# A mixer, a mixture of experts and two attention layers on one core: the experts' weights used unsplit, in two halves of TensorE's columns

## The reference, cut to what matters

```python
x = x + gt1 * y_x                                   # token mixer
tokens = rms_norm(x, g_norm2) * (1.0 + sc2) + sh2
y = moe_ffn(tokens, ...)                            # 16 experts, 2 for a token
x = rms_norm(x + gt2 * y, g_final)
for l in range(2):                                  # second_block
    x = x + merged(delta, sparse, memory) @ w_out[l]
    x = x + (silu(gt) * up) @ w_ffn_out[l]
return rmsnorm(x, norm_final)
```

## Time and profile before

| | |
|---|---|
| three runs | 2695.44, 2700.69, 2703.59 us, median 2700.69 |
| the profiled execution's own time | 2700.96 us |
| its span in the profile | 2699.1 us |
| busy: PE, DVE, ACT, POOL | 2580.8, 1887.9, 1511.8, 181.7 us |
| moved by DMA | 610.09 MB |
| mixer and routing | to about 448 us |
| experts | about 448 to 1190 us |
| two layers | about 1193 to 2682 us |
| end | to 2699.1 us |

### The profile page before, as it was taken

How to read it: one execution, slowest core, us unless ns; L and a number is a source line. 1 busy time by engine, 2 the same in 40 slices (tenths; PEclk the granted TensorE clock), 3 DMA queues, 4 the chain that set the end, 5 groups by cost and what they waited for, 6 DMA issues and landing times.

```text
span 2699.1 us, 44061 instructions
## 1 busy us (share of the span) xinstructions
PE 2580.8 (96%) x16251; PEld 2173.3 (81%) x16251; DVE 1887.9 (70%) x2149; ACT 1511.8 (56%) x1543; POOL 181.7 (7%) x211
## 2 busy tenths in 40 slices
PE   5999998999999999999999999999999999999997
PEld 3756887878787878879897787899898977878995
DVE  3444767999999999975677575555456785756553
ACT  4433555888888888863556453443345564533432
POOL 0000010000000000000074000000000740000000
PEclk9999998999999999999999999999999999999999
DMA  7434636999999999964433025454544340254545
GB/s 284 161 151 157 225 141 256 400 413 407 408 411 405 411 403 413 403 275 169 156 144 138 34 102 203 172 188 160 193 171 146 140 152 34 102 203 172 188 156 195
DMA packets 79658, 610.09 MB, mean 226 GB/s; under 512 B 16004, under 2 KB 21700, under 8 KB 24968
## 3 DMA queue, kind: packets, MB, share of 16 engines
q1 hardware_dynamic: 79496, 607.87, 58.3%
HBM read 606.79 MB, written 1.05 MB: 225 GB/s over the span
## 4 chain that ended last, share of the span: by engine, by line
issue 48%; PE 33%; DVE 8%; POOL 6%; DMA 2%; ACT 2%; SPq 1%; DVEq 0%; POOLq 0%; ACTq 0%
PE psum_scalar L1801 4%; PE psum_scalar L1802 4%; DVE weight_slabs_rounded L1759 3%; PE psum_vector L550 3%; PE psum_vector L552 3%; PE psum_vector L551 3%; POOL arena L3543 3%; PE psum_scalar L550 2%; PE psum_scalar L551 2%; PE psum_scalar L552 2%; POOL arena L3546 2%; DVE arena_rounded L1759 2%; PE psum_vector L1773 2%; DMA weight_slabs<-in_mixer_slabs 1%; PE psum_scalar L1841 1%
## 5 line engine op out<-in xcount | busy, mean ns | idle before, releaser
L2202 DVE TENSOR_TENSOR weight_slabs_rounded<-weight_slabs,arena_rounded 128x2048 fp32r<-128x2048 f32 x208 | 477.9, 2307 | 342.5 <-ACT arena_rounded L2199 293.2
L2199 ACT ACTIVATE arena_rounded<-weight_slabs 128x2048 fp32r<-128x2048 f32 x208 | 396.4, 1913 | 361.6 <-PE psum_vector L552 223.5
L550 PE MATMUL psum_scalar<-arena_rounded,arena_rounded 128*128 128x256 f32 (+1 forms) x1456 | 472.6, 325 | 20.1 <-DVEq L1294 7.5
L550 PE MATMUL psum_vector<-arena_rounded,arena_rounded 128*128 128x512 f32 (+3 forms) x1264 | 456.2, 361 | 15.0 <-DVE weight_slabs_rounded L2202 14.9
L1759 DVE TENSOR_TENSOR weight_slabs_rounded<-weight_slabs,arena_rounded 128x2048 fp32r<-128x2048 f32 x192 | 430.9, 2285 | 9.0 <-DVE arena L1978 3.9
L1747 ACT ACTIVATE arena_rounded<-weight_slabs 128x2048 fp32r<-128x2048 f32 x192 | 362.2, 1910 | 38.5 <-PE psum_scalar L1802 19.8
L552 PE MATMUL psum_vector<-arena_rounded,arena_rounded 128*128 128x512 f32 (+1 forms) x896 | 348.0, 388 | 0.0
L551 PE MATMUL psum_vector<-weight_slabs_rounded,arena_rounded 128*128 128x512 f32 x880 | 343.8, 391 | 0.0
L550 PEld LDWEIGHTS psum_scalar<-arena_rounded,arena_rounded 128*128 128x128 f32 x1456 | 278.7, 191 | 52.4 <-issue 22.3
L1801 PE MATMUL psum_scalar<-arena_rounded,arena_rounded 128*128 128x512 f32 x768 | 307.9, 401 | 2.7
L550 PEld LDWEIGHTS psum_vector<-arena_rounded,arena_rounded 128*128 128x128 f32 (+2 forms) x1264 | 237.9, 188 | 54.6 <-DVE weight_slabs_rounded L2202 11.5
(11 more groups left out here) (497 smaller groups left out, 4138.8 us busy)
## 6 DMA issues: line engine op xcount, KB each, us to landing
weight_slabs<-in_layer_slabs SPq DMA_DIRECT2D x103, 2048.0 KB, 7.7
weight_slabs<-in_expert_slabs SPq DMA_DIRECT2D x192, 1024.0 KB, 8.2
arena<-in_expert_slabs SPq DMA_DIRECT2D x96, 1024.0 KB, 8.5
weight_slabs<-in_mixer_slabs SPq DMA_DIRECT2D x32, 2048.0 KB, 8.3
weight_slabs<-in_layer_slabs SPq DMA_DIRECT2D x6, 1024.0 KB, 5.5
arena<-in_mem SPq DMA_DIRECT2D x3, 1024.0 KB, 11.9
arena<-in_b_gate SPq DMA_DIRECT2D x6, 512.0 KB, 8.3
arena<-in_x SPq DMA_DIRECT2D x1, 1024.0 KB, 5.2
```

Of the source, the lines that this page charges most:

```text
L550: pe.matmul(out, left[0], right[0], start=start, stop=False)
L2199: e.activation(fr(high), low, ACT.Copy).then_inc(S("weights_high"), 1)
L2202: e.tensor_tensor(fr(low), low, fr(high).bitcast(F32), ALU.subtract).then_inc(S("weights_split"), 1)
```

## The change

Experts' weights are no longer split. `xgT` and `actT` hold the 64 tokens once, in float32. PE multiplies them with the float32 weights; even chunks k go to the upper 64 partitions of the bank, odd ones to the lower, each matmul with 64 stationary columns (`half_rows`). ACT copies the lower 64 partitions, DVE adds both halves, ACT takes silu, DVE multiplies, and four transposes (`act_to_T`) take the place of the eight matmuls of `folded`. The down product's two halves stay apart, and `combine` adds them as before. ACT's and DVE's operations at L1747 and L1759 are gone.

The room of the high parts becomes places for weights: 16 places instead of nine. Halves 16 and 17 lie where 7 and 8 lay. The first loads are spread over earlier waits, and g_final comes behind them.

```diff
+            sp.wait_ge(*mix_spent[29])
+            first_expert(4, 5, 8)
+            sp.wait_ge(*mix_spent[30])
+            first_expert(0, 1)
+            sp.wait_ge(S("x_columns"), 2 * NT)
+            first_expert(2, 3, 6, 7, 9, 10, 11, 12, 13)
+            sp.wait_ge(S("squares"), ROOTS_SO_FAR - 1)
+            first_expert(14, 15)
+            sp.wait_ge(S("routing"), 2)
+            sp.dma_start(gfin, a["g_final"].partition_broadcast(P)).then_inc(S("final_gain_in"), 16)
...
+            def block(i, *behind):
+                this, following = expert_of(i), expert_of(i + 1)
+                halves_of(following, i + 1, *range(7))
+                halves_of(this, i + 1, 16, 17)
+                halves_of(following, i + 1, *behind)
+
+            with sp.Fori(0, last_) as i:
+                block(i, *range(7, 16))
+            halves_of(expert_of(last_), last_ + 1, 16, 17)
...
+        def expert_before(h):
+            return {16: 7, 17: 8, 7: 16, 8: 17}.get(h, h)
```

```diff
-                        pe.matmul(bank, xgT[:, k, :], high[:, k % 4], start=k == 0, stop=False)
-                        mm = pe.matmul(bank, xgT[:, k, :], low[:, k % 4], start=False, stop=k == KC - 1)
+                        mm = pe.matmul(bank[half_rows(k), :], xgT[:, k, :], weights[:, k % 4], start=k < 2, stop=k >= KC - 2)
...
+                for n in range(3):
+                    both_halves(gate_sum)
+                    both_halves(act, wait=True)
+                    e.wait_ge(S("gact_ready"), 3 * i + n + 1)
+                    tt(act[0:SLOTS, :], act[0:SLOTS, :], gate_sum[0:SLOTS, :], ALU.mult).then_inc(S("act_ready"), 1)
```

Behind the experts, ACT makes the first two high parts of the second block after the last result, and DVE makes the first low part after x has been added to, the second after the final norm:

```diff
-            Splitter(e, 0, high=False).upto(1)
...
             e.sem_inc(S("x_expert"), 1)
+            first_layer = Splitter(e, 0, high=False)
+            first_layer.upto(0)
...
             e.sem_inc(S("x_ready"), 1)
+            first_layer.upto(1)
```

Idle float32 products of 512 columns, which nobody reads, are put on PE at three places: eight before the wait for routing, two and one before the transposes of the sparse attention's weights in each layer, and four before the wait for the norm that leads to the feed-forward part:

```diff
+        def idle_products(pe, n):
+            for _ in range(n):
+                pe.matmul(pst[:, :], ident, cst[:, 0:BANK], start=True, stop=True)
...
+            idle_products(pe, 8)
             pe.wait_ge(S("routing"), 1)
...
+                    idle_products(pe, 2 - g)
                     probs_to_T(at)
...
+                idle_products(pe, 4)
                 pe.wait_ge(S("diagonals_ready"), 2 * l + 2)
```

The layers' hardware loops become two copies of the code (`for l in range(2)`), and the second copy leaves out the memory rows, the three slabs and the splits for a layer that does not exist. norm_final is loaded during the second feed-forward part. The last down product finishes the rows of the first 128 tokens first, and adding, squaring, scaling and storing go by 128 tokens:

```diff
-                for k in range(FC):
+                for pair in range(0, FC, 2):
...
+                    rows_first = pair == FC - 2
...
-            sp.wait_ge(S("layer_free"), 4)
-            sp.dma_start(out.rearrange("(t p) d -> p t d", p=P), x).then_inc(S("stored"), 16)
+            for t in range(NT):
+                sp.wait_ge(S("layer_free"), 3 + t)
+                sp.dma_start(out[t * P:(t + 1) * P, :], x[:, t, :]).then_inc(S("stored"), 16)
```

More of the change, by code:

```diff
@@ L1668, in sp_moe, with first_expert, expert_of, halves_of @@
         def sp_moe(sp):
-            m = parts["moe"]
             def load(h, src):
[L1673 to L1691, removed]
+                sp.dma_start(expert_half(h).rearrange("p k n -> p (k n)"), src).then_inc(half_arrived(h)[0], 16)
+            def first_expert(*halves):
+                for h in halves:
+                    at = h % 2 * 4 * BANK
+                    load(h, a["expert_slabs"][0, h // 2, :, at:at + 4 * BANK])
+            sp.wait_ge(*mix_spent[29])
[8 more added lines that the diff above has]
+            sp.dma_start(gfin, a["g_final"].partition_broadcast(P)).then_inc(S("final_gain_in"), 16)
+            last_ = last_block(sp)
+            def expert_of(i):
+                return sp.value_load(ids[0:1, bass.ds(i, 1)], min_val=0, max_val=NE - 1)
+            def halves_of(expert, i, *halves):
+                for h in halves:
+                    half_read(sp, i, expert_before(h))
                     sp.sem_inc(S("slot_seen_free"), 1)
@@ L1695, in block @@
                     load(h, src[:, at:at + 4 * BANK])
[L1697 to L1715, removed]
@@ new lines, in half_arrived @@
+        def half_arrived(h):
+            place = place_of(h)
+            if place >= 13:
+                return S(f"expert_half{place}"), 0
+            if place >= 6:
+                name, earlier = (("constants_in", 16), ("x_in", 16), ("ctx_in", 16), ("c_in", 32), ("sgu_in", 16),
+                                 ("ln_rows_in", 32), ("late_rows_in", 16))[place - 6]
+                return S(name), earlier
+            if place % 2 == 0:
+                return parts["moe"][f"slab{place // 2}"], 0
+            return parts["mix"][f"slab{place // 2}"], 16 * len([n for n in range(len(MIX_SLABS)) if n % 3 == place // 2])
@@ L1737, in half_read @@
                 e.wait_ge(m["slab_used"], 11 * i + (h // 2 + 1 if h < 12 else h - 5))
[L1739 to L1759, removed]
         def pe_moe(pe):
@@ L1869, in act_moe @@
             e.preload_act_table(ACT.Silu)
-            for h in range(3):
-                expert_high(e, 0, h)
             last_ = last_block(e)
@@ L2003, in one_block, with both_halves @@
-                low_parts(16)
-                actT_low(2)
-                low_parts(17)
-                if last:
-                    return
-                expert_halves(e, False, i + 1, (0, 1, 2))
-                assert step.n == MOE_STEP and V.n == MOE_V, (step.n, V.n)
+                def both_halves(dst, wait=False):
+                    n = A.n
+                    b = A.take()
+                    e.wait_ge(S("lower_half"), 6 * i + n + 1)
+                    A.give(tt(dst[0:SLOTS, :], b[0:SLOTS, :], lower_halves[n % 2][0:SLOTS, :], ALU.add), wait=wait)
@@ L2011, in vec_moe @@
+                assert last or step.n == MOE_STEP, step.n
             with e.Fori(0, last_) as i:
@@ L2196, in upto @@
                         before = half_before(g)
-                        if before is not None and (before >= 0 or not isinstance(self.l, int)):
+                        if before is not None and LH * self.l + before >= 0:
                             half_spent(e, self.l, before)
@@ L2795, in squares @@
                 e.sem_inc(S("squares"), 1)
-            with e.Fori(0, 2) as l:
+            for l in range(2):
                 A = Banks(e, psa, m["scalar_full"], m["scalar_free"], base=LAY_A * l, looped=True)
```

318 lines of the change are left out of this document (141 added, 177 removed).

## The result

| | before | after |
|---|---|---|
| median | 2700.42 us (6 runs, 2695.44 to 2703.59) | 2711.36 us (6 runs, 2708.66 to 2716.69) |
| ratio | | 1.0046, 95% interval 1.0032 to 1.0060 |
| span of the profiled execution | 2699.1 | 2711.6 |
| busy: PE, DVE, ACT | 2580.8, 1887.9, 1511.8 | 2533.5, 1283.1, 1019.3 |
| last combine starts | 1189.99 | 1220.61 |

A forecast was written before the change was run, and what follows sets the result against it. PE bounded an experts' block by a hair (46.24 us); after the change DMA would, with a period of 49.1. 2700.96 + 19.9 (experts) + 7.6 (behind them) - 15.0 (layers and end) = 2713.5 us, range 2685 to 2725.

The forecast's parts named there:

- Products without a split: Experts' blocks: float32 products in two column halves run together, 0.86 us a pair; PE's block takes 39.9 us.
- The hole: Experts' loads: half 7 waits until 16 is read; DMA loses 2.5 us a block, slow clock makes the period 49.1.
- The last case among the chances: Experts' loads: 17 read slowly too, so 8 late behind 7; period up to 50.8, total 2720 to 2736 us; chance 0.08.
- The start of the experts: Routing before the experts: block 0 starts at 441.4 us, as idle products fill a 6.87 us wait, saving 6.6.
- with the clock kept: Routing: after the idle products, PE's products from 431.0 to 448.06 us lose their half pace; 6.6 us on PE's path.
- Sum for the experts: Experts' stage: thirteen periods of 49.1 us, combine at 1209.9 against 1189.99, so +19.9 us.
- Behind the experts: From combine into layer 0: PE starts 10.8 us after combine instead of 3.1; third half 24.7 instead of 17.1, +7.6.
- The layers and the end: Layers: norm -3.4, transposes -1.4, memory rows -2.1, loop's return -2.4; kernel's end -5.7; together -15.0 us, bounds -9 and -20.
- the first: Rival, experts' loop: the clock stays up, period 47.4 us, total 2689.9 us; chance 0.23.
- DMA is not quicker: Rival judged, experts' loads: DMA runs at 433 GB/s instead of 420, total 2695 us; chance 0.11.
- The halves overlap: Rival judged, experts' products: the halves do not overlap, a block takes 70.8 us, total 3087 us; chance 0.03.
- the half-true one: Rival, experts' loads: the change does not do what it says, as loads are not in reading order; no chance given.

The follow-up runs named there:

- experiment 1: Kernel after the change, with the next expert's weight halves 9 and 10 loaded ahead of 7 and 8: 2640.95 us, ratio 0.9785 to the kernel before.
- experiments 1 and 2: The second of these: kernel after the change, with only half 9 loaded ahead of 7 and 8: 2674.27 us, ratio 0.9898 to the kernel before.
- Experiment 3: Kernel after the change, with seven idle products on PE ahead of the wait for half 16, in all blocks but the last: 2698.87 us, ratio 0.9991.
- experiment 5: Kernel after the change, with the second block's first splits made before the last expert result (ACT) and before the wait for combine (DVE): 2706.86 us, ratio 1.0023.
- Experiments 5 and 8: The latter: kernel after the change, with the edits of experiment 1 and experiment 5 together: 2634.88 us, ratio 0.9762 to the kernel before.
- experiment 6: Kernel after the change, without any of its idle products, in routing and in the layers: 2718.93 us, ratio 1.0060 to the kernel before.

## Why the prediction was right, and where it was not

The forecast was 2713.5 and the result 2711.4, by the mechanism that it named: the hole behind half 16, the granted clock at 0.50 in it, once in each block. But two of its sums were off by 11 us each and cancelled.

**Products without a split.** Right: two halves run together, 0.86 us a pair. PE's block is 40.5 (block 0, without a wait, 40.52 in experiments 1 and 2), not 39.9; it binds nowhere. That DVE and ACT lose a third of their work bought nothing, as forecast.

**The hole.** Right in kind, shown by the first two experiments: with the queue filled the last combine comes 68.9 us earlier, of 70 in the total. Its size is 49.72 - 44.89 = 4.8 us, forecast 4.2 (2.5, and 1.7 for the clock). Experiment 3 parts it: 1.7 for the clock, as forecast, 3.1 for the rest, within the bounds of 1.9 to 3.2 but not the 2.5 taken. Where the difference lies is seen in the landing of single loads (the view of the loads' line, narrowed to the one issue of half 7 at 533.55, then to that of half 8 at 535.88):

```profile
DMA to landing us min/median/max: 5.0/5.0/5.0
...
DMA to landing us min/median/max: 6.0/6.0/6.0
```

Half 7, behind an empty queue, needs the 5.0 us that were counted (5.0 to 5.5 in all 14 blocks), and over the 14 blocks it lands 9.1 us behind half 16 (forecast 9.2); in experiment 3, at full clock, 7.45 (forecast 7.5). So that path was right. The step that failed is the one behind it: the sum lets 8 follow 7 back to back, 2.49 us later, and it lands 3.3 us behind it on average (2.5 to 4.2), in experiment 3 3.1. With the fifteen loads from there to the next 16 the period is 9.1 + 3.3 + 15 x 2.494 = 49.8. The last case among the chances, 8 late behind 7 because 17 is read slowly too, had named this term with 0.08. It is only half true: at full clock 8 is still 0.6 late. It is issued 2.3 us behind 7, soon enough, but needs 6.1 us from issue to landing on average where 7 needs 5.1; why, no run shows.

**The start of the experts.** Wrong: block 0 at 441.4, measured 444.59. The failed step is "with the clock kept". The idle products fit the wait only at the full granted clock; they took 8.04 us instead of 6.9, because the clock had fallen before them (PEclk 0.69 from 421 to 423 us, 0.50 from there to 425; L933 takes 2.66 us, the same 16 records took 1.94 in the kernel before), so they themselves held the next product up by 1.5. And the clock did not stay: it was granted in full from 425.5 to 435.2 us and at 0.50 from 435.6 to 442.0, behind the small products of the routing, so L1782 still took 4.88 against 3.59. Worth 1.7 instead of 6.6.

**Sum for the experts:** +30.6 measured, +19.9 forecast. Of the 10.7, 8.1 are 13 periods of 49.72 instead of 49.1, 0.7 the last block, and 1.9 stand already at the first wait (529.6, forecast 527.7). In these 1.9 the late start is 3.2, less 2.5 for a slip of the sum: it put 17 loads between half 7 and the next 16, where its own period has 16. Of the other 1.2, 0.8 is half 8 again and 0.4 is block 0's own length.

**Behind the experts.** Right: PE starts 10.9 after combine, 10.8 forecast, and the lag against the kernel before stays at 38.5 us into the layers, 7.9 more than at combine (+7.6). Experiments 5 and 8 give 6.6 and 8.0 back.

**The layers and the end.** -25.9 measured, -15.0 forecast. Idle products before the norm 1.6 a layer (1.7 forecast), the loop's return 2.4 (2.4), memory rows about 2 (2.1), as forecast; at the transposes 1.7 a layer instead of 0.7, of which chance is a part. The end gave 8.0, not 5.7: norm_final is worth less than 2.9 on its own; DVE's last split, for a layer that does not exist, had held up the adds, which the prediction called off the path, and the store is 1.3 shorter. That is 19 of the 25.9. Another 5 are one place, the chain of 64-row products in layer 1, and some 2 lie scattered over the layers. Its last two steps before and after:

```profile
2283.45 1.51 PE L2568 MATMUL psum_scalar<-arena 64*64 64x64 f32 x49 [0.95 <-issue]
...
2288.77 1.29 PE L2568 MATMUL psum_scalar<-arena 64*64 64x64 f32 x48 [0.82 <-DVE arena L3382]
2290.42 0.83 PE L2568 MATMUL psum_scalar<-arena 64*64 64x64 f32 x16 [0.36 <-ACT arena L2997]
2291.18 5.27 PE L2654 MATMUL psum_scalar<-arena 128*128 128x128 f32 x32
```

```profile
2310.26 2.40 PE L2528 MATMUL psum_scalar<-arena 64*64 64x64 f32 x59
...
2315.43 2.17 PE L2528 MATMUL psum_scalar<-arena 64*64 64x64 f32 x59
2317.63 3.84 PE L2614 MATMUL psum_scalar<-arena 128*128 128x128 f32 x32
```

The waits of up to 0.95 us are gone, and the 32 records behind them take 3.84 at a granted clock of 1.00 (2317 to 2321 us) instead of 5.27, of which 2292 to 2294 us at 0.50. From the first of these products to behind them it is 5 us, in no step of the prediction, which had given the two copies of the layer's code only the loop's return. The longest wait is named "issue", so the profile doesn't show what PE waited for. In all runs without the hardware loop the 256 products of the chain take 16.5 to 17.7 us in layer 1, 19.9 before. But in layer 0, where the same loop is gone, they take 16.9 to 21.0 us, 20.4 before, and all but experiment 6's keep waits of 0.6 to 1.5 us there. The packed traces have one thing more: in all ten, each of the 21 waits of 0.5 us and more in front of these products ends 1.2 to 1.9 us behind the end of a 16 KB transfer on the instruction queue (before: 2282.15 and 2283.45, 1537.44 and 1538.82), and so does the wait at the loop's return (1938.78, 1940.47). Instructions that come late would fit. But transfers with no wait behind them stand there as well, and no run changed this; nor was a kernel with the loop kept and all else changed tried. The cause stays open.

**The rivals.** The granted clock does fall, to 0.50, in all 14 blocks with waits of 5.6 to 8.0 us, so the first is out. But the ground given for it, that a wait of 2.44 us leaves no trace and every one of 3.37 or more does, doesn't hold: experiment 1 has a slow half 16 after 2.45 us and a full pace after 3.37, experiment 5 slow products after 1.80. DMA is not quicker: with the hole filled 420 GB/s and 44.89 us a block stand, where 433 would be 43.6. The halves overlap. And the half-true one, that the order is not the order of reading, is what the first experiment repaired.

## What to carry to other kernels

When loads go out in a fixed order, look for the one that waits for a reader, and count what is still queued when that reader begins. The queued loads and the blocked one together must last as long as reading, issue and landing: here 4 x 2.49 = 10.0 us against 9.1, with three loads of 1 MB queued instead of one, for 70 us. Free places did not help while their loads stood behind a blocked one: those of 9 to 15 did so here, and each block lost 4.8 us. And a forecast that lands on the number can be two errors; the boundaries between stages, compared one by one, are what shows it.

## What was not expected of the hardware

Products for different column halves overlapped even when they were not neighbours, some two matmuls ahead (8.9 us for 16 matmuls, where overlap of neighbours alone would give 11.1). Idle products placed where the granted clock had already fallen (0.50 from 423 to 425 us) ran slowly themselves and cost part of what they were to save (8.04 instead of 6.9 us). The first load into an empty queue landed in 5.1 us and the second took a microsecond more, though it was issued in time. A granted clock of 0.50 behind a wait for DMA cost nothing where DMA's queue was not empty: the kernel of the first experiment has it in 8 of its 14 waiting blocks and keeps DMA's floor (44.89 us a block), and which blocks have it doesn't follow the length of the wait (slow after 2.45 us, at full pace after 3.37).
